# Shift and scale rows kept on chip, in two passes, with the row loads reshaped and the parameter work moved

## The reference, cut to what matters

```
def modulation(cvec, w_mod, b_mod):
    m = jax.nn.silu(cvec) @ w_mod + b_mod            # [2048] @ [2048, 6 * 2048]
    return m[..., None, :]

def trunk_layer(x, mod, ...):
    sh1, sc1, g1, sh2, sc2, g2 = jnp.split(mod, 6, axis=-1)
    h = rmsnorm(x, lp['g_pre1']) * (1 + sc1) + sh1
    t, k, v, h_fin = token_mixer(h, ...)             # h @ w_in, recurrence, attention, output projections
    x = x + g1 * rmsnorm(t, lp['g_post1'])
    h = rmsnorm(x, lp['g_pre2']) * (1 + sc2) + sh2
    f = expert_choice_ffn(h, ...)                    # 16 experts
    x = x + g2 * rmsnorm(f, lp['g_post2'])
```

## Time and profile before

| | us |
|---|---|
| median of 3 runs | 3074.99 (3066.91 to 3075.38) |
| the profiled execution | 3073.05 |
| its span on the core | 3071.3 |

### The profile page before, as it was taken

One profiled execution on the slowest core, in us unless ns is written; L12 is line 12 of the kernel. 1 busy time (PEld: TensorE's weight loads), 2 busy tenths in 40 slices (PEclk: granted clock), 3 DMA queues, 4 the chain that ended last, 5 costly groups with the idle time before them and its releaser, 6 DMA issues.

```text
span 3071.3 us, 42461 instructions
## 1 busy us (share of the span) xinstructions
PE 2905.0 (95%) x15704; PEld 2316.1 (75%) x15704; DVE 2144.0 (70%) x1829; ACT 1532.9 (50%) x1459; POOL 290.1 (9%) x357
## 2 busy tenths in 40 slices
PE   6899999999899999989999995999999999999993
PEld 2489999998788888879997774666666666666662
DVE  6635797885666666663334457788888888888886
ACT  5651212222455555552223343677777777777773
POOL 1000000002111111100000000010100000010100
PEclk9999999999999999999999997999999999999997
DMA  9646696685333333334333564899999999999995
GB/s 358 224 154 221 192 296 211 213 286 156 111 115 114 114 114 114 117 133 137 116 112 131 197 240 173 318 376 378 383 382 390 385 386 388 386 375 384 378 397 219
DMA packets 293206, 758.25 MB, mean 247 GB/s; under 512 B 20496, under 2 KB 184936, under 8 KB 228344
## 3 DMA queue, kind: packets, MB, share of 16 engines
q1 hardware_dynamic: 266768, 638.80, 57.4%
q0 software_dynamic: 23936, 102.69, 10.2%
q10 hardware_dynamic: 2432, 15.83, 1.3%
HBM read 700.99 MB, written 56.25 MB: 247 GB/s over the span
## 4 chain that ended last, share of the span: by engine, by line
PE 81%; DVE 8%; DMA 4%; issue 3%; ACT 2%; POOL 0%; DVEq 0%; SPq 0%; POOLq 0%; ACTq 0%
PE ps L419 15%; PE ps L420 15%; PE ps L421 15%; PE ps L1802 8%; PE ps L1803 7%; PE ps L1804 7%; DVE mod_acc L1262 3%; PE ps L1936 2%; PE ps L1938 2%; PE ps L1937 2%; PE ps L1727 2%; PE ps L1865 1%; PE ps L1887 1%; PE ps L1849 1%; DMA raw<-in_w_mod 1%
## 5 line engine op out<-in xcount | busy, mean ns | idle before, releaser
L374 DVE TENSOR_TENSOR we_lo<-raw,we_hi 128x2048 fp32r<-128x2048 f32 x384 | 876.3, 2290 | 140.0 <-ACT we_hi L369 139.0
L369 ACT ACTIVATE we_hi<-raw 128x2048 fp32r<-128x2048 f32 x384 | 736.4, 1918 | 288.4 <-PE ps L421 288.4
L1802 PE MATMUL ps<-hi,w_lo 128*128 128x320 f32 x2048 | 647.0, 316 | 9.0 <-DVE w_lo L349 4.8
L1804 PE MATMUL ps<-hi,w_hi 128*128 128x320 f32 x2048 | 634.3, 310 | 0.0
L1803 PE MATMUL ps<-lo,w_hi 128*128 128x320 f32 x2048 | 634.1, 310 | 0.0
L349 DVE TENSOR_TENSOR w_lo<-raw,w_hi 128x2048 fp32r<-128x2048 f32 (+1 forms) x184 | 351.0, 1919 | 249.5 <-ACT w_hi L340 242.5
L340 ACT ACTIVATE w_hi<-raw 128x2048 fp32r<-128x2048 f32 (+1 forms) x184 | 294.4, 1612 | 294.4 <-PE ps L421 182.4
L1802 PEld LDWEIGHTS ps<-hi,w_lo 128*128 128x128 f32 x2048 | 385.9, 188 | 27.6 <-issue 14.5
L419 PE MATMUL ps<-we_hi,xs_lo 128*80 128x512 f32 x1024 | 402.6, 393 | 2.2 <-DVE xs_lo L1658 2.2
L420 PE MATMUL ps<-we_lo,xs_hi 128*80 128x512 f32 x1024 | 403.1, 394 | 0.0
L421 PE MATMUL ps<-we_hi,xs_hi 128*80 128x512 f32 x1024 | 400.5, 391 | 0.0
(11 more groups left out here) (340 smaller groups left out, 3748.2 us busy)
## 6 DMA issues: line engine op xcount, KB each, us to landing
raw<-in_w_e_gate SPq DMA_DIRECT2D x128, 1024.0 KB, 7.2
raw<-in_w_e_up SPq DMA_DIRECT2D x128, 1024.0 KB, 7.3
raw<-in_w_e_down SPq DMA_DIRECT2D x128, 1024.0 KB, 12.3
raw<-in_w_in SPq DMA_DIRECT2D x144, 512.0 KB, 5.2
mod_raw<-in_w_mod SPq DMA_DIRECT2D x64, 1024.0 KB, 5.3
raw<-in_w_mod SPq DMA_DIRECT2D x64, 512.0 KB, 5.1
raw<-in_w_o SPq DMA_DIRECT2D x64, 512.0 KB, 4.7
d_proj<-stage POOLq DMA_DIRECT2D x32, 320.0 KB, 3.3
```

What stands on the lines that cost most here:

```text
L369: act.activation(we_hi[:, k % NEH, :], raw_slot(k), ACT.Copy).then_inc(hi_ready, 2)
L374: TTn(we_lo[:, k % NEH, :], raw_slot(k), we_hi[:, k % NEH, :].bitcast(F32), ALU.subtract).then_inc(lo_ready, 2)
L1802: pe.matmul(out, wl, hi[:, k, ms], start=(k % 16 == 0), stop=False)
L1804: last = pe.matmul(out, wh, hi[:, k, ms], start=False, stop=(k == KT - 1))
```

## The change

The rows of shift and scale no longer pass through DRAM, and six things go with that.

1. High and low parts of the conditioning vectors stand side by side in `c_hl`, four stationary columns. A tile is multiplied by it in two passes, low part and high part, so four result rows appear: two from the high, two from the low columns. (The product low by low, left out before, is now in the sum.)
2. The first group uses banks 4 to 7, the second 0 to 3.
3. The four rows are copied to SBUF (`m_row0`, `m_row1`), half by VectorE and half by ScalarE; TensorE turns them in sixteen pieces of 4 x 128, and VectorE adds bias and the two kinds of rows in columns. The bias comes in with `rows1`.
4. The turns of the first group stand after the second group's second tile, the tokens' turns one tile later than before.
5. Each weight tile's two loads are now 64 partitions by 2048 columns instead of 128 partitions by 1024.
6. The parameter work stands inside the value projection, on ScalarE after the first tile of its second column block, on VectorE after the same tile.

```diff
-        def by_halves(pe, u, slot, out, s_hi, s_lo, start, stop):
+        def by_halves(pe, u, slot, out, c, start, stop):
 
             for p in range(2):
                 pe.wait_ge(lo_ready, 2 * NRAW + 2 * u + p + 1)
                 for n in (2 * p, 2 * p + 1):
                     s = slice(n * 512, (n + 1) * 512)
-                    last = three(pe, out[:, n, :], s_hi, s_lo, w_hi[:, slot, s], w_lo[:, slot, s], start, stop)
+                    pe.matmul(out[:, n, :], c, w_lo[:, slot, s], start=start, stop=False)
+                    last = pe.matmul(out[:, n, :], c, w_hi[:, slot, s], start=False, stop=stop)
                 last.then_inc(halves_used, 1)
...
             with sp.Fori(0, 2) as g:
                 for k in range(KT):
                     load(Q_MOD + g * 4 + k // NRAW, k % NRAW,
-                         [(raw[:, k % NRAW, s], src) for s, src in rows(w_mod, k, g * D)])
+                         [(raw[r:r + HD, k % NRAW, :], w_mod[k * P + r:k * P + r + HD, bass.ds(g * D, D)]) for r in (0, HD)])
...
             pool.memset(A["zero"][:], 0.0).then_inc(pool_own, 1)
             pool.wait_ge(pool_own, 1)
 
-            def mod_group(g):
-                wait(pool, "m_row_ready", g)
-                plain()
-                pool.dma_start(A["b_row"][:], a["b_mod"][0:1, bass.ds(g * D, D)].to_broadcast([2, D])
-                               ).then_inc(S["b_loaded"], 16)
-                wait(pool, "m_row_ready", g + 1)
-                plain()
-                pool.dma_start(d_mod[:, bass.ds(g * D, D)], A["m_row"][:]).then_inc(S["m_stored"], 16)
-                stored("m_stored", (g + 1) * 16, "m_row_free")
-
-            for g in range(2):
-                mod_group(g)
-                for r in range(2):
-                    at_row = 32 * r + 16 * g
-                    pool.dma_start(A["rows3"][at_row:at_row + 16, :], flat(d_mod[r, g * D:(g + 1) * D])
-                                   ).then_inc(S["rows3_loaded"], 16)
             leave(pool)
             for t in range(TT):
...
+            def mod_half(g):
+
+                act.wait_ge(halves_used, used((Q_MOD + g * 4 + 4) * 4))
+                b = 6 - 4 * g
+                act.activation(A[f"m_row{g}"][:, 1024:2048].rearrange("p (b n) -> p b n", b=2), ps[0:4, b:b + 2, :], ACT.Copy
+                               ).then_inc(S["row_act"], 1)
+
+            for k in range(KT):
+                split_hi(act, Q_MOD + 4, k + 1, fine=True)
+                if k == 0:
+                    mod_half(0)
+                if k % 3 == 0 and k < 3 * TT:
+                    square(k // 3)
+                if k % 3 == 0 and k:
+                    take_x(k // 3 - 1)
+            mod_half(1)
+            leave(act)
+            for kq in range(4):
+                for k in range(4 * kq, 4 * kq + 4):
+                    if k % 8 == 0:
+                        act.wait_ge(S["a1_ready"], k // 8 + 1)
+                    tokens(k)
+                split_hi(act, Q_V, kq + 1)
             act.wait_ge(S["small_dve"], 1)
             act.activation(A["lams"][0:1, 2:4], A["lams"][0:1, 0:2], ACT.Exp).then_inc(S["small_act"], 1)
             act.wait_ge(S["small_dve"], 2)
             act.activation(A["sp_b"][:], A["sp_a"][:], ACT.Exp, scale=-1.0).then_inc(S["small_act"], 1)
...
+            def mod_columns(g, h):
+
+                dve.wait_ge(S["rows3_turned"], 2 * g + h + 1)
+                r = ps[:, 4 + 2 * h, 0:32].rearrange("p (k r) -> p r k", r=4)
+                n = 16 * g + 8 * h
+                dst = A["cols3"][:].rearrange("p (v n) -> p v n", v=2)[:, :, n:n + 8]
+                own.done(TTn(dst, r[:, 0:2, :], A["cols1"][:, None, 48 + n:56 + n].to_broadcast([P, 2, 8]), ALU.add))
+                own.settle()
+                own.done(TTn(dst, r[:, 2:4, :], dst, ALU.add))
+                if g:
+                    own.settle()
+                    STT(A["A1"][:, :, 8 * h:8 * h + 8], dst, 1.0, A["cols1"][:, None, 32 + 8 * h:40 + 8 * h].to_broadcast([P, 2, 8]),
+                        ALU.add, ALU.mult).then_inc(S["a1_ready"], 1)
...
             for k in range(KT):
                 split_lo(dve, Q_MOD, k + 1, fine=True)
+            for k in range(KT):
+                split_lo(dve, Q_MOD + 4, k + 1, fine=True)
+                if k == 0:
+                    mod_half(0)
+                if k == 1:
+                    mod_columns(0, 0)
+                    mod_columns(0, 1)
+                if k % 3 == 1 and k < 3 * TT:
+                    norm_diagonal(k // 3)
+                if k % 3 == 0 and k:
+                    take_x(k // 3 - 1)
+            mod_half(1)
+            mod_columns(1, 0)
+            mod_columns(1, 1)
+            dve.sem_inc(S["mod_used"], CREDIT["mod_used"])
+            leave(dve)
+
+            def take_values(c):
+                wait(dve, "v_free", c)
+                for t in range(TT):
+                    if t < TT - 1:
+                        dve.wait_ge(S["bank_done"], c * (TT - 1) + t + 1)
+                    else:
+                        dve.wait_ge(halves_used, used((Q_V + c + 1) * 4))
+                    dve.tensor_copy(v_stage[:, t, :], ps[:, t, :]).then_inc(S["bank_taken"], 1)
+
+            for kq in range(4):
+                for k in range(4 * kq, 4 * kq + 4):
+                    tokens(k)
+                split_lo(dve, Q_V, kq + 1)
             dve.wait_ge(S["rows_turned"], 2)
-            dve.tensor_copy(A["cols2"][:], ps[:, 7, 128:233]).then_inc(S["cols_ready"], 1)
-
+            dve.tensor_copy(A["cols2"][:], ps[:, 5, 0:105]).then_inc(S["cols_ready"], 1)
...
             take_values(0)
             for kq in range(4):
                 split_lo(dve, Q_V + 1, kq + 1)
+            dve.wait_ge(S["lam_spread"], 1)
+            own.done(dve.tensor_copy(lam_col, ps[:, 7, 0:1]))
             take_values(1)
...
             def mod_group(g, after=()):
 
-                wait(pe, "m_row_ready", g)
+                b = 4 - 4 * g
                 for k in range(KT):
-                    by_halves(pe, Q_MOD * NRAW + g * KT + k, k % 2, ps[0:2, 0:4, :], c_hi[:, k, :], c_lo[:, k, :],
-                              k == 0, k == KT - 1)
+                    by_halves(pe, Q_MOD * NRAW + g * KT + k, k % 2, ps[0:4, b:b + 4, :], c_hl[:, k, :], k == 0, k == KT - 1)
                     if k in after:
                         after[k]()
 
-            def turn_vectors():
-                pe.wait_ge(S["rows3_loaded"], 64)
-                turn(ps[:, 7, 0:64], A["rows3"][:], 64).then_inc(S["rows3_turned"], 1)
+            def turn_rows(g):
+
+                if g:
+                    pe.wait_ge(S["xt_act"], 2 * TT)
+                for h in range(2):
+                    if h == 0:
+                        wait(pe, "m_row_ready", g + 1)
+                    else:
+                        pe.wait_ge(S["row_act"], g + 1)
+                    for k in range(8):
+                        last = turn(ps[:, 4 + 2 * h, 4 * k:4 * k + 4], A[f"m_row{g}"][:, (8 * h + k) * P:(8 * h + k + 1) * P], 4)
+                    last.then_inc(S["rows3_turned"], 1)
 
             def turn_parameters():
                 pe.wait_ge(par_loaded, N_PAR * 16)
-                turn(ps[:, 7, 128:233], A["rows2"][:], 105).then_inc(S["rows_turned"], 1)
+                pe.wait_ge(S["xt_dve"], 2 * TT)
+                turn(ps[:, 5, 0:105], A["rows2"][:], 105).then_inc(S["rows_turned"], 1)
 
             def spread_lambda():
                 pe.wait_ge(S["lam_val"], 1)
-                pe.matmul(ps[:, 6, 0:1], A["ones_row"][:], A["lams"][0:1, 5:6], start=True, stop=True
+                pe.matmul(ps[:, 7, 0:1], A["ones_row"][:], A["lams"][0:1, 5:6], start=True, stop=True
                           ).then_inc(S["lam_spread"], 1)
 
             pe.wait_ge(S["c_ready"], 1)
-            mod_group(0, {8: turn_parameters})
-            spread_lambda()
-            mod_group(1, {3 * t + 1: (lambda t=t: turn_x(t)) for t in range(TT)})
-            turn_vectors()
+            mod_group(0)
+            turns = {3 * t + 2: (lambda t=t: turn_x(t)) for t in range(TT)}
+            turns[1] = lambda: turn_rows(0)
+            mod_group(1, turns)
+            turn_rows(1)
+            turn_parameters()
             leave(pe)
...
                      lambda k: pe.wait_ge(S["tok_lo"], k + 1) if c == 0 else None)
+                if c == 0:
+                    spread_lambda()
```

More of the change, by code:

```diff
@@ L160, in trunk @@
         xT = at("xT", [P, KT, N_TOK], F32, rb)
-        A = place(s0, [("b_row", [2, D], F32), ("m_row", [2, D], F32), ("junk0", [P, D], F32),
-                       ("zero", [P, D], F32), ("rows1", [48, P], F32), ("rows2", [105, P], F32),
-                       ("rows3", [64, P], F32), ("cols1", [P, 48], F32), ("cols2", [P, 105], F32),
+        A = place(s0, [("m_row0", [4, D], F32), ("m_row1", [4, D], F32), ("junk0", [P, D], F32),
+                       ("zero", [P, D], F32), ("rows1", [80, P], F32), ("rows2", [105, P], F32),
```

(55 more changed lines are left out.)

24 lines of the change are left out of this document (11 added, 13 removed).

## The result

The changed kernel takes 3108.1 us (median of 4, 3106.6 to 3114.2) where the kernel before takes 3073.8: ratio 1.012, 95% interval 1.0099 to 1.014. It is slower by 34 to 37 us; 20 were forecast. The measured time is inside the stated range (3051 to 3110), near its top. The ratio, taken of the 3075 that the forecast started from, would put it at 3112, just past it.

The account below looks back on a forecast made before the run. Loads were to set the pace up to the value projection: weights 133, zeros 13, token tiles 13, first bytes 3.3 give 162.5 us; 13 more, start 175.5, +21. Forecast 3094 to 3095 us, range 3051 to 3110.

Parts of the forecast that it names:

- Part 5: Weight loads of both groups: 64 partitions by 8 KB rows would run at 252 GB/s, against 407 before.
- full rate: Rival, weight loads: halves overlap at 407 to 423 GB/s, start 19 us earlier, 3054 to 3056 us; chance 0.37.
- The sum: Up to the value projection: load times plus the way behind them, start at 175.5 instead of 154.5, +21 us.
- 33.6 MB of weights: Loads of both groups: all 32 weight tiles at 252 GB/s take 133 us.
- token tiles: Loads beside the weights: five token tiles, 5.24 MB at 407 GB/s, take 13 us.
- zeros: GpSimd's five zero stores to d_f: 5.24 MB at 394 GB/s occupy all DMA engines for 13 us.
- first bytes: Kernel start: the first loaded bytes arrive at 3.3 us.
- last landing to projection: Behind the last weight tile: splits, copies, turns, columns and token tile take 13 us.
- Parts 1 to 3: Both groups and tail: second group 55 us instead of 64.0, stall gain 6.7, tail gain 6.6, if loads allow.
- the tail: From the second group's last product to the projection: 5.4 us instead of 12.0, gain 6.6.
- Part 4: GpSimd's zero stores, unnamed by the change, would move from 152 to about 10 us, onto busy DMA engines.
- Half rate: Rival, weight loads: halves strictly alternate at 212 GB/s, start +46 us, about 3120 us; chance 0.12.

Follow-up runs that it names:

- e1: The changed kernel with each weight tile loaded as before, in two halves of 128 partitions by 1024 columns: 3055.6 us, ratio 0.9945.
- e2: The kernel before with only its weight loads of the first two groups made 64 partitions by 2048 columns: 3111.6 us, ratio 1.0122.
- e3: The changed kernel with each tile's two loads taking even and odd partitions, still 64 rows of 8 KB: 3056.2 us, ratio 0.9951.
- e8: The changed kernel, half-height loads kept, with GpSimd's zero stores held until the projection can start: 3105.2 us, ratio 1.0112.
- e5: The changed kernel with column-half loads and GpSimd's zero stores held until the projection can start: 3049.1 us, ratio 0.992.
- e10: The changed kernel with lower halves of tiles loaded by SP, upper halves by GpSimd, zero stores behind them: 3091.8 us, ratio 1.006.
- e7: The changed kernel with column-half loads and a third product for each 512 columns put back: 3068.9 us, ratio 0.9985.

## Why the prediction came out as it did

**Part 5, the cause: right, and chosen by a hair.** It had a chance of 0.38 against 0.37 for full rate. One edit (e1) removes the whole loss and 17 us more; the same edit alone (e2) slows the kernel before by 39 us; keeping row and load sizes but spreading the partitions (e3) is as good as e1.

**The sum: right in its form, wrong in three terms.** I had the last tile landed at 162.5; it was split at 175.2, and that is the difference between +21 and +33.

| term | forecast | measured |
|---|---|---|
| 33.6 MB of weights | 133 (252 GB/s) | 142 (236, window 100 to 160) |
| token tiles | 13 (407 GB/s) | 22 (5.24 MB at the flow's 235, e8) |
| zeros | 13 | 4.4 in the start (e8) |
| first bytes | 3.3 | 3.3, taken over |
| last landing to projection | 13 | 12.6 |

142 + 22 + 4.4 + 3.3 = 172, 3 short of the 175. The rest is in the bytes: from 2 us to 175.2 the trace has 260 GB/s, 45.0 MB, and the sum counts 44.0; the difference is the small parameter loads and, most likely, the first bytes of the value projection's tile, issued at 165. The step that failed is the sentence "I take 252 GB/s for these loads": the gather windows give the rate of the whole flow, ordinary loads in it too, and I used it for the weights alone while pricing everything beside them at 400. Read as what it was, 44 MB at 252 is 175 us, the last landing at 178 and the projection at about 191; measured were 175.2 and 187.8. In the table's terms the weights were 9 us and the token tiles 9 us too cheap, and the zeros 9 us too dear. That the 252 came within 7% of the 236 was in part luck: it is the rate of a gather mixed with ordinary loads, and no run before the change had measured the loads that it stood for.

**Parts 1 to 3: right, and hidden.** The stall between the groups is gone. At full rate (e1) the second group takes 54.7 us (55 forecast, 51 to 58), the tail 5.6 (5.4), the projection starts at 137.8 (135.4) and the time is 3055.6 (3054 to 3056). Put back, the third product costs 13 us in time. Whether moving the parameters alone matters was not tried by itself; the timeline above shows them covered by 1.15 us. One small price was wrong: a turn of the row took 0.07 us and not 0.14, so eight cost 0.6 and not 1.1.

**Part 4: right that they move, and it was worth naming.** They went at 20 us and not at 10, as told above. At full load rate the early zeros cost 9 us of start (e5); beside half-height loads 4.

**Rivals.** Full rate was the change's other possible outcome and its working was good to 2.4 us, but the condition was not met: the loads ran at 236, the threshold was 326. Half rate, 212, gave 3120, as far above the measured time (12 us) as the forecast was below it (13); its rate was too low. By the 218 GB/s of the Trainium skill (SBUF — State Buffer, "Door 1: The DMA port swizzle") for the weights, the forecast's own method gave +42, an estimate. Measured were +33, and the rate was 236.

## What to carry to other kernels

Let one DMA load reach partitions below 64 and from 64 up alike. Splitting a tile by partition halves to get longer rows cost 42% of the load rate here, while splitting by columns, by odd and even partitions, or not at all ran at 408 to 425 GB/s. When a transfer of a new shape joins a busy queue, price the whole flow at the slow rate, not that transfer alone. And when waits are removed from an engine's program, look at what stood behind them: GpSimd's zero stores moved by 130 us into the busiest stretch, and holding them back was worth 6 us at full load rate.

## What the runs showed of the hardware

- Half-height loads one after the other moved 234 to 236 GB/s (223 from 10 to 30 us in e8) with all DMA engines shown busy; the busy share says nothing of the rate (1.02 at 236, 1.02 at 408).
- Stores from SBUF to DRAM beside them raised the flow to 339; loads of 128 partitions hardly did (235, at most 242).
- TensorE's granted clock averaged 0.75 of 2.4 GHz from 48 to 175 us and 0.63 in e10's window 60 to 100, with TensorE busy 58% of the time there; at that load it set no pace. Some products then ran at the lower level of 1.2 GHz: in the change around 55 us, after 4.9 us of idle TensorE, they start 0.43 us apart instead of 0.23.
- A product with four stationary columns took as long as one with two: 403 to 412 ns in e7's window 80 to 144, 403 to 410 in the second group before.
- A turn of 4 x 128 took 1.12/16 = 0.07 us, half of what the turns of 80 x 128 in the earlier trace rows took.
